# Later turned weights made by GpSimd in the state space loop, and an attention order with all projection pieces behind the odd head's first logits

## The reference

```python
def forgetting_attention(h, w_in, b_f, w_out):
    q, k, v, f_logit = split(h @ w_in)            # 16 heads of 64
    c = cumsum(log_sigmoid(f_logit + b_f))
    p = softmax(causal(q @ k.T * scale + c_i - c_j))
    return (p @ v) @ w_out

def s5_layer(h, w_in, ...):
    u = h @ w_in                                  # 64 groups of 16 channels
    s_t = lam_bar * s_(t-1) + b_bar @ u_t         # 64 complex states a group
    y = real(c_mat @ s_t) + d * u
    g = gelu(y)
    return val * sigmoid(gate)                    # val, gate = split(g @ w_glu)
```

## Time and profile before

| what | value |
|---|---|
| median of 3 runs | 4047.77 us (4044.93 to 4048.03) |
| profiled execution | 4043.6 us, span 4041.8 us |
| mean granted TensorE clock | 0.944 of full speed |
| busy shares | PE 92%, PEld 71%, VectorE 51%, ScalarE 27%, GpSimd 26% |
| DMA | 346.08 MB, mean 86 GB/s |
| forgetting attention | about 91 to 305 us and 1934 to 2146 us |
| state space layer | about 738 to 954 us, its loop from 849 us |
| latent attention | about 2813 to 2878 us, and once more near 3580 us |

### The profile page before, as it was taken

The page is one execution under the profiler, slowest core; times in us unless marked ns, Lnnn a source line. Parts: engine busy times, 40 slices in busy tenths (PEclk is TensorE's granted clock), DMA queues, the critical chain, the costliest instruction groups (busy, mean ns, idle before and its releaser), DMA issues. The chain is left out here.

```text
span 4041.8 us, 44371 instructions
## 1 busy us (share of the span) xinstructions
PE 3704.8 (92%) x16819; PEld 2882.5 (71%) x16819; DVE 2070.9 (51%) x2631; ACT 1079.9 (27%) x1480; POOL 1069.0 (26%) x835
## 2 busy tenths in 40 slices
PE   7889999958999979999888999997899999879999
PEld 6657888736788858887666888762678877347887
DVE  4446554775554475455445545565443356454334
ACT  4432122023222222123442212333222223332121
POOL 0443634600363326350342635001200000130000
PEclk9889999978999989999888999988999999889999
DMA  3105444122444334442112444310133321012332
GB/s 109 46 21 126 128 123 116 54 63 65 115 136 121 108 87 126 129 118 80 53 32 77 136 129 120 87 34 21 42 94 97 89 81 55 21 32 83 88 104 78
DMA packets 554319, 346.08 MB, mean 86 GB/s; under 512 B 33270, under 2 KB 535420, under 8 KB 554172
## 3 DMA queue, kind: packets, MB, share of 16 engines
q1 hardware_dynamic: 540348, 293.79, 25.9%
q0 software_dynamic: 13824, 50.34, 4.3%
HBM read 341.01 MB, written 3.08 MB: 85 GB/s over the span
## 5 line engine op out<-in xcount | busy, mean ns | idle before, releaser
L1273 PE MATMUL ps<-h_hi,w_hi 128*128 128x512 f32 x2880 | 1154.4, 401 | 51.4 <-DVE h_lo L1194 15.4
L1274 PE MATMUL ps<-h_lo,w_hi 128*128 128x512 f32 x2880 | 1137.5, 395 | 0.0
L1275 PE MATMUL ps<-h_hi,w_lo 128*128 128x512 f32 x2880 | 1136.0, 394 | 0.0
L1235 DVE TENSOR_TENSOR w_lo<-w,w_hi 128x2048 fp32r<-128x2048 f32 (+2 forms) x294 | 663.7, 2258 | 165.3 <-ACT w_hi L1228 163.2
L1228 ACT ACTIVATE w_hi<-w 128x2048 fp32r<-128x2048 f32 (+2 forms) x294 | 507.0, 1725 | 711.0 <-PE ps L1275 639.9
L1273 PEld LDWEIGHTS ps<-h_hi,w_hi 128*128 128x128 f32 x2880 | 551.4, 191 | 175.9 <-issue 56.3
L1275 PEld LDWEIGHTS ps<-h_hi,w_lo 128*128 128x128 f32 x2880 | 550.2, 191 | 117.5
L1274 PEld LDWEIGHTS ps<-h_lo,w_hi 128*128 128x128 f32 x2880 | 551.5, 191 | 110.2 <-issue 0.5
L1364 DVE TENSOR_TENSOR sg<-sg,ps 128x512 f32<-128x512 f32 x132 | 90.8, 688 | 719.3 <-ACT sg L1349 719.3
L1273 PE MATMUL ps<-a_hi,w_hi 128*128 128x512 f32 x1056 | 412.0, 390 | 0.0
L1275 PE MATMUL ps<-a_hi,w_lo 128*128 128x512 f32 x1056 | 411.0, 389 | 0.0
(11 more groups left out here) (471 smaller groups left out, 4018.8 us busy)
## 6 DMA issues: line engine op xcount, KB each, us to landing
w<-in_ffn_w_gate_up SPq DMA_DIRECT2D x176, 512.0 KB
w<-in_w_ada POOLq DMA_DIRECT2D x96, 512.0 KB, 7.0
w<-in_ffn_w_down SPq DMA_DIRECT2D x64, 704.0 KB
w<-in_w_gate_up SPq DMA_DIRECT2D x88, 512.0 KB
w<-in_w_down SPq DMA_DIRECT2D x32, 704.0 KB
w<-in_fox_w_in SPq DMA_DIRECT2D x32, 512.0 KB
w<-in_w_in SPq DMA_DIRECT2D x14, 1024.0 KB
w<-in_fox_w_in SPq DMA_DIRECT2D x8, 1024.0 KB
```

The costliest lines, as they stand in the source:

```text
L1235: last = nc.vector.tensor_tensor(lo, raw, hi.bitcast(F32), ALU.subtract)
L1273: nc.tensor.matmul(out, hi, a[0][:, k, :], start=k == 0, stop=False)
L1274: nc.tensor.matmul(out, hi, a[1][:, k, :], start=False, stop=False)
L1275: return nc.tensor.matmul(out, lo, a[0][:, k, :], start=False, stop=k == kt - 1)
```

## The change

State space loop: `turn_w(q + 2)` stands between `inputs(q + 1)` and `outputs(q)` (q from 1) in place of `turn_w(q + 3)` behind `outputs(q)`. ScalarE copies these weights ahead of the copy of y. Weights 3 to 7 are made by GpSimd, behind its loop for `v0`, each set once the set before is turned; VectorE keeps weights 0 to 2. Attention: in the odd head, pieces 4 and 5 stand behind the first tile's logits and 6 and 7 behind the second's, `times_v` is the last thing in the head, and `stage_high` for the next head comes behind the weights' split and so before the third exponential. VectorE's place for `stage_low` (behind the third maximum) stays.

```diff
         for q in range(DK):
             if q + 1 < DK:
                 inputs(q + 1)
+            if 3 <= q + 2 < DK:
+                turn_w(q + 2)
             outputs(q)
-            if q + 3 < DK:
-                turn_w(q + 3)
             if q:
                 turn_y(q - 1)
...
         for q in range(DK):
+            if 3 <= q + 2 < DK:
+                weights(q + 2)
             e.wait_ge(m.sem["y_done"], m.at("y_done", q + 1))
...
-            if q + 3 < DK:
-                weights(q + 3)
...
+        for q in range(3, DK):
+            e.wait_ge(m.sem["wt_turned"], m.at("wt_turned", q))
...
+            r, i, t = (four(a) for a in self.wt)
+            tt(r, b[0], w[0], ALU.mult)
+            tt(i, b[0], w[1], ALU.mult)
+            m.pool(e, tt(t, b[1], w[1], ALU.mult))
+            m.pool(e, tt(r, r, t, ALU.subtract))
+            m.pool(e, tt(t, b[1], w[0], ALU.mult))
+            tt(i, i, t, ALU.add).then_inc(m.sem["wp_ready"], 1)
+            e.wait_ge(m.sem["wp_ready"], m.at("wp_ready", q - 2))
...
             if q + 1 < DK:
                 scan(q + 1)
-            if q + 3 < DK:
-                weights(q + 3)
             if q >= 2:
                 low(q - 2)
...
             self.logits(e, s, 0)
+            self.project(e, p, () if even else (4, 5))
             self.logits(e, s, 1)
-            self.project(e, p, () if even else (4, 5))
+            self.project(e, p, () if even else (6, 7))
             if s:
                 self.turn(e, s - 1, 0)
                 self.turn(e, s - 1, 1)
-            if not even and s >= 3:
-                self.times_v(e, s // 2 - 1)
             self.logits(e, s, 2)
-            self.project(e, p, (0, 1) if even else (6, 7))
+            self.project(e, p, (0, 1) if even else ())
             if s:
                 self.turn(e, s - 1, 2)
             self.logits(e, s, 3)
             self.project(e, p, (2, 3) if even else ())
             if s:
                 self.turn(e, s - 1, 3)
+            if not even and s >= 3:
+                self.times_v(e, s // 2 - 1)
...
                     if t == 1:
                         self.ahead(e, p, "scalar")
-                    if t == 2:
                         self.stage_high(e, s + 1)
```

More of the change, by code:

```diff
@@ L70 @@
     biased s5_rows s5_step s5_loaded s5_act c_loaded c_turned ct_ready5 ut_done ug_ready ug_half pw_ready v0_ready blk_ready
-    tap_done k_ready k_stored t0_loaded t1_loaded t2_loaded wt_ready wt_turned wl_ready sin_done sin_taken y_done y_taken yt_done h_done angles second_loaded sines conv_ready acs_ready
+    tap_done k_ready k_stored t0_loaded t1_loaded t2_loaded wt_ready wp_ready wt_turned wl_ready sin_done sin_taken y_done y_taken yt_done h_done angles second_loaded sines conv_ready acs_ready
     cb_ready acsT_ready xdtd_ready bt_ready2 st_ready am_ready decay_ready xdt_ready l_ready sc_ready
@@ L809, in turn_w @@
         def turn_w(q):
-            e.wait_ge(m.sem["wt_ready"], m.at("wt_ready", q + 1))
+            if q < 3:
+                e.wait_ge(m.sem["wt_ready"], m.at("wt_ready", q + 1))
+            else:
+                e.wait_ge(m.sem["wp_ready"], m.at("wp_ready", q - 2))
             if q:
@@ L971, in gpsimd @@
             e.wait_ge(m.sem["v0_ready"], m.at("v0_ready", q + 1))
+        for q in range(3, DK):
+            e.wait_ge(m.sem["wt_turned"], m.at("wt_turned", q))
+            b = [self.bb[a][:, 64 * q:64 * q + 64].rearrange("p (r k c) -> p r k c", r=4, k=1).broadcast_to([P, 4, S5_L, C5]) for a in range(2)]
+            w = [self.pq[a][:, 4 * q:4 * q + 4, :].rearrange("p r (k c) -> p r k c", c=1).broadcast_to([P, 4, S5_L, C5]) for a in range(2)]
+            r, i, t = (four(a) for a in self.wt)
[5 more added lines that the diff above has]
+            tt(i, i, t, ALU.add).then_inc(m.sem["wp_ready"], 1)
+            e.wait_ge(m.sem["wp_ready"], m.at("wp_ready", q - 2))
     def vector(self, e):
@@ L1114, in end @@
         finish(self.m, w_hi_ready=1, quad_taken=self.n, ut_done=DK, ug_ready=DK, ug_half=DK, h_ready=DK,
-               v0_ready=DK, blk_ready=DK, tap_done=DK, k_ready=2, k_stored=16 * 3, t0_loaded=128 * 3, t1_loaded=128 * 3, t2_loaded=128 * 2, wt_ready=DK, wt_turned=DK, wl_ready=DK, sin_done=DK,
+               v0_ready=DK, blk_ready=DK, tap_done=DK, k_ready=2, k_stored=16 * 3, t0_loaded=128 * 3, t1_loaded=128 * 3, t2_loaded=128 * 2, wt_ready=3, wp_ready=DK - 3, wt_turned=DK, wl_ready=DK, sin_done=DK,
                sin_taken=DK, st_ready=DK, y_done=DK, y_taken=DK, yt_done=DK, h_done=DK, pads_clear=1)
```

## The result

After: 4000.39 us median (3990.42 to 4002.48, 4 runs), beside 4046.35 us for the kernel before (4028.09 to 4048.03, 4 runs); ratio 0.9892, 95% interval 0.9859 to 0.9925. Forecast was 4021, range 4004 to 4036: the sign was right, the size was not.

What follows compares the result with a forecast made beforehand. In the loop TensorE and VectorE wait in turn; in the attention TensorE waits for the staged low part, its clock falling. Terms -17.7, -9.1, +3.8, -1.0, -2.4 make -26.4: 4047.8 to 4021 us, range 4004 to 4036.

Steps and rivals of the forecast that it cites:

- State space loop: Scan 2 starts sooner (-6.0), four rounds shorten (-16.6), GpSimd delays VectorE ahead of the loop (+4.9): -17.7 us.
- without them and the waits: Loop's four further rounds: without making weights and without waits, a round is 6.6 us, before 4.1 us of SBUF meeting.
- the ring: Loop: TensorE's turning waits for VectorE's weights, VectorE's scan for inputs behind that turning; rounds of 14.85 us against 6.6.
- The row: Earlier trace, VectorE beside GpSimd in SBUF: a 128x256 operation goes from 0.42 to 1.28 us, 0.85 more.
- rival 2: State space loop: the lock costs GpSimd's whole operation, rounds of 14.0 us, total 4037 us; chance 0.14.
- Odd heads: Forgetting attention: even head's first logits wait for the gate at T = 12.0, not 12.2; 0.76 us each, twelve places, -9.1 us.
- at the end: Forgetting attention's last head: `times_v` behind the last logits, last turn some 0.5 us sooner; -1.0 us for both.
- Head 1: Forgetting attention, no `times_v` there: gate at 11.85, the exponential behind it later; +1.9 us, twice, +3.8 us.
- Latent heads: Latent attention: VectorE's third maximum no longer waits 3.51 us, little reaches the turn; 1.2 us a stage, -2.4 us.
- places in the attention where the clock does not fall any more: Listed sign of a wrong forecast: TensorE's clock stays up inside the attention, each place worth up to 2.4 us.
- Rival 3: Attention gives nothing, since the gate is as late or the lower clock eats the 0.76 us; 4030 us, chance 0.13.
- Rival 1: Nothing meets in SBUF: state space -34, attention -8.7, total 4005 us; chance 0.12.

Runs made afterwards that it cites:

- s5_vector: Kernel before with only the state space loop's new TensorE and ScalarE order, all weights left on VectorE: 4028.3 us, ratio 0.9946.
- best: Kernel after with all weights on VectorE and forgetting-attention head 1 in the old order of pieces and `stage_high`: 3990.8 us, ratio 0.9862.
- values_high: Kernel before with `times_v` last in odd heads from the third and `stage_high` a tile earlier, pieces in old places: 3999.1 us, ratio 0.9885.
- values_pieces: Kernel before with pieces early and `times_v` last in odd heads, `stage_high` still behind tile 2: 4025.7 us, ratio 0.9958.
- best_values: Kernel before with only `times_v` last in odd heads from the third and the later turning, weights on VectorE: 3976.4 us, ratio 0.9841.
- att_pieces: Kernel before with the attention's early pieces and early `stage_high`, `times_v` in its old place: 4050.3 us, ratio 1.0012.
- att_values: Kernel before with only `times_v` moved behind the last logits in every odd head from the third: 3998.0 us, ratio 0.9880.
- att_filler: Kernel before, order kept, with unread products ahead of each attention's last turns (eight) and last `times_v` (four): 4032.0 us, ratio 0.9964.

## Why the prediction was wrong in size, point by point

- **State space loop: the sum nearly right (-17.7, measured -19.8), its cause only half.** By the starts of the scans' first operation, as the forecast counted: from scan 1 to 2 -7.0 (forecast -6.0). The next four rounds: 10.7 us in the mean (10.7), though no two alike (11.7, 14.1, 6.6, 10.5): -16.4 (-16.6). The round of 14.1 us meets most of two of GpSimd's sets, the one of 6.6 us hardly any, so that the mean came out to a tenth is in part luck. Ahead of the loop the gather is 4.4 us later (4.9). Not forecast: the round behind, 7.8 instead of 6.6 us, and 1.9 us less in the tail. The meeting in SBUF, taken from the earlier trace rows as 4.1 us a round, measured 17.1 / 4 = 4.3. What failed is the sentence ahead of the sum, "without them and the waits": I booked the gain to what VectorE is spared. `s5_vector` gives as much with VectorE spared nothing. The gain is the ring's end; the spared work is paid back in SBUF, 17.1 us in the loop and 4.4 ahead of it for 19.2.
- **The lock.** VectorE's scans beside GpSimd's operations take 1.43 to 1.70 us instead of 0.69. By the Trainium skill (SBUF — State Buffer, "SBUF: two separate sides") the loser fully blocks. A single pair of operations can look like that: in the kernel before, L1035 (128x32) takes 1.27 us in the two places where one of GpSimd's two-input operations (L968, L969) runs and 0.19 us in its four others, 1.08 us more, though it has an eighth of the elements of the operations in the earlier trace rows, which pay 0.85. Over the loop the cost was 0.71 us for each GpSimd operation of 1.26. That is less, as I read it, because in part of the time VectorE has operations that were not stretched, the four on PSUM among them. The row was the better price, and rival 2 fell.
- **Odd heads: forecast 0.76 us, measured 1.0; timing almost exact.** The third maximum was put at T = 8.97 (8.78), the gate's end at 11.95 (11.76), the even head's first logits at 12.0 (11.86). So the chain was read rightly for the whole change. What I did not ask is what each of its parts does. The forecast has the pieces make the second tile's logits 2.85 us late as a given, and sets `times_v` last down as work that hides. In fact the one costs 1.9 us a head (0.9 where `stage_high` is early too) and the other gives 1.8. The even heads, which the forecast left alone, gave 0.4 us in one attention and nothing in the other, and lie between 12.6 and 14.0 us. Of the -1.0 us "at the end" nothing is seen up to the last reciprocal: the last head went from 9.41 to 9.05 us in one attention and from 8.63 to 9.05 in the other.
- **Head 1: forecast +1.9, measured +1.8.** With that head alone in the old order it was gone (`best`, 10.36), and `values_high` (10.38) beside `values_pieces` (13.0) puts it on the pieces.
- **Latent heads: -2.0 against -2.4**, near by luck. Odd heads took 7.31 us instead of 7.78 and the last head 7.13 instead of 7.80, 1.6 us a stage where 1.2 was forecast. Head 1, whose code the change leaves alone, took 0.8 and 0.6 us more, as it does in some kernels with the old order (6.6 to 7.4).
- **The step that failed: the stretch behind each attention, put at nothing, measured -11.9 us.** The forecast has -1.0 us "at the end" and looks no further than the last turn. It even names "places in the attention where the clock does not fall any more, each worth up to 2.4 us", but as a sign of being wrong and inside the attention. They were behind it: over all kernels run, the stretch was 61.8 to 63.7 us in 24 places of 24 with `times_v` in its old place and no filler (mean 62.9), and with `times_v` last in every odd head, without filler, 58.5 to 58.7 in 17 places of 28, 60.1 to 60.2 in 6 and 63.4 to 63.5 in 5 (mean 59.8). Which of the three comes was not foreseen anywhere: shifts elsewhere in the kernel change it, as the unchanged latent code in `best` (63.50) and `best_values` (58.65) shows.
- **The rest of the gap** between -41 (spans) and -46 (medians) is the scatter of the kernel before: its medians lay between 4041.6 and 4047.8 in six sets, and its profiled execution 4.2 us beneath the first of them. The 41.1 us of the spans alone, taken off the forecast's 4047.8, would have lain just inside the range, at 4006.7.

Rival 3, "the attention gives nothing", was right of the pieces (`att_pieces`: ratio 1.0012) and wrong of the change. Rival 1 gave nearly the time that came, 4005, for a reason that did not hold.

Open: the clock's pattern inside the attentions, with even heads between 12.5 and 14.0 us before and after and 12.4 to 12.8 in `att_values`, was not taken apart. Over heads 0 to 15 of the first forgetting attention it was 0.85 before, 0.86 after, 0.90 in `att_values` and 0.92 in `best_values`, whose even heads take 11.2 to 14.0 us.

## What to carry to other kernels

Where a change has several parts that go the same way, cost each part alone, against the rows with only that part in: here one move was worth more than the whole, and another took it back. When two engines take turns, look for the ring and open it once; moving the work as well pays only if the second engine does not cost the first as much as it spares it. And end the account not where the moved instructions end but at the next stage's first full-speed product: what TensorE does in its last microseconds can decide at which clock the next stage begins, as the filler of `att_filler` shows.

## What the runs showed of the hardware

- VectorE lost 0.71 us to each GpSimd operation of 1.26 us (17.1 us over 24, GpSimd's all SBUF to SBUF). A copy with one SBUF input is stretched too: L1087 took 1.02 and 1.14 us in the loop, the same copy 0.28 us in `s5_vector`.
- TensorE's clock fell to its lower level behind two gaps of 2.37 and 1.11 us in 24 places of 24, and behind gaps of 1.88 and 1.11 us in some and not in others; twelve bf16 products that nobody reads, put into the longer ones, kept it at 2.4 GHz up to the next gap (2.55 us) and were worth 1.4 to 3.1 us a place.
